# Causal attention: one visit for the values of a pair of heads, and the filling projections at other places

## The reference

```python
def mla_attention(c_q, c_kv, k_rope, q_norm, w_uq, kv_norm, w_ukv, cos, sin):
    q = (rmsnorm(c_q, q_norm) @ w_uq).reshape(b, s, MLA_HEADS, QK_NOPE + QK_ROPE)
    ...
    kv = (rmsnorm(c_kv, kv_norm) @ w_ukv).reshape(b, s, MLA_HEADS, QK_NOPE + V_DIM)
    k_nope, v = kv[..., :QK_NOPE], kv[..., QK_NOPE:]
    ...
    for i in range(s // Q_BLOCK):
        q0 = i * Q_BLOCK
        kend = q0 + Q_BLOCK
        sc = (jnp.einsum('bqhd,bkhd->bhqk', q_nope[:, q0:kend], k_nope[:, :kend])
              + jnp.einsum('bqhr,bkr->bhqk', q_pe[:, q0:kend], k_pe[:, :kend]))
        ...
        pr = jax.nn.softmax(jnp.where(mask, sc, -jnp.inf), axis=-1).astype(v.dtype)
        outs.append(jnp.einsum('bhqk,bkhd->bqhd', pr, v[:, :kend]))
```

## Time and profile before

| | us |
|---|---|
| median of 3 runs | 3806.12 (3800.87 to 3807.11) |
| profiled execution, its own time | 3797.35 |
| its span, first to last instruction | 3795.5 |
| TensorE busy in the span | 3663.5 |
| causal attention, layer 0, about | 201 to 341 |

### The profile page before, as it was taken

One profiled execution on the slowest core, in us unless ns is written; L12 is line 12 of the kernel. 1 busy time (PEld: TensorE's weight loads), 2 busy tenths in 40 slices (PEclk: granted clock), 3 DMA queues, 4 the chain that ended last, 5 costly groups with the idle time before them and its releaser, 6 DMA issues.

```text
span 3795.5 us, 58344 instructions
## 1 busy us (share of the span) xinstructions
PE 3663.5 (97%) x19742; PEld 2985.5 (79%) x19742; DVE 2165.3 (57%) x3292; ACT 1860.3 (49%) x3571; POOL 1772.5 (47%) x1395
## 2 busy tenths in 40 slices
PE   8999899999999988999999999999999999999999
PEld 7866688788888666887888887778888987678887
DVE  4567642788535676427885764742235957743234
ACT  4555544444445555444344545744444653754443
POOL 4423573556544235735565453065563235025564
PEclk9999999999999999999999999999999999999999
DMA  4210241455222102414553322132223542012222
GB/s 143 89 62 29 73 139 62 155 190 187 94 89 89 62 29 73 145 62 153 195 183 106 128 95 95 46 106 96 97 95 104 174 161 78 2 43 91 94 95 88
DMA packets 106907, 388.48 MB, mean 102 GB/s; under 512 B 11856, under 2 KB 11984, under 8 KB 106320
## 3 DMA queue, kind: packets, MB, share of 16 engines
q1 hardware_dynamic: 87840, 318.81, 24.5%
q10 hardware_dynamic: 16416, 57.62, 4.4%
q0 software_dynamic: 2448, 9.36, 0.7%
HBM read 383.64 MB, written 2.10 MB: 102 GB/s over the span
## 4 chain that ended last, share of the span: by engine, by line
PE 69%; issue 15%; DVE 7%; POOL 6%; ACT 2%; DMA 0%; POOLq 0%; ACTq 0%; DVEq 0%; SPq 0%
PE ps L676 18%; PE ps L678 18%; PE ps L677 18%; POOL arena_parts L640 3%; PE ps L1163 2%; POOL arena_parts L644 1%; PE ps L1182 1%; PE ps L1171 1%; DVE rstd L2135 1%; PE ps L2200 1%; POOL lines L431 1%; PE ps L1141 1%; PE ps L2210 1%; PE ps L907 1%; PE ps L848 1%
## 5 line engine op out<-in xcount | busy, mean ns | idle before, releaser
L677 PE MATMUL ps<-arena_parts 128*128 128x512 f32 (+1 forms) x3156 | 1174.3, 372 | 0.0
L640 POOL TENSOR_TENSOR arena_parts<-ring,arena_parts 128x512 fp32r<-128x512 f32 x492 | 655.5, 1332 | 1021.4 <-ACT arena_parts L617 817.8
L676 PE MATMUL ps<-h_parts,arena_parts 128*128 128x512 f32 x2096 | 822.8, 393 | 10.1 <-POOL arena_parts L640 7.2
L678 PE MATMUL ps<-h_parts,arena_parts 128*128 128x512 f32 x2096 | 816.6, 390 | 0.0
L644 POOL TENSOR_TENSOR arena_parts<-ring,arena_parts 128x512 fp32r<-128x512 f32 x492 | 664.7, 1351 | 282.2 <-ACT arena_parts L626 281.6
L677 PEld LDWEIGHTS ps<-arena_parts 128*128 128x128 f32 x3156 | 596.1, 189 | 104.3 <-issue 2.4
L1663 DVE SCALAR_TENSOR_TENSOR conv<-ps,cols,conv 128x511 f32<-128x511 f32 (+3 forms) x536 | 377.6, 705 | 525.0 <-ACT conv L1678 371.3
L617 ACT ACTIVATE arena_parts<-ring 128x512 fp32r<-128x512 f32 x574 | 361.2, 630 | 640.5 <-PE ps L678 595.0
L626 ACT ACTIVATE arena_parts<-ring 128x512 fp32r<-128x512 f32 x574 | 360.2, 628 | 589.4 <-PE ps L678 553.2
L676 PEld LDWEIGHTS ps<-h_parts,arena_parts 128*128 128x128 f32 x2096 | 394.3, 188 | 97.0 <-POOL arena_parts L640 8.1
L678 PEld LDWEIGHTS ps<-h_parts,arena_parts 128*128 128x128 f32 x2096 | 394.2, 188 | 82.4
(11 more groups left out here) (357 smaller groups left out, 6450.4 us busy)
## 6 DMA issues: line engine op xcount, KB each, us to landing
ring<-in_stream SPq DMA_DIRECT2D x606, 512.0 KB, 3.2
ctx<-in_mod ACTq DMA_DIRECT2D x48, 512.0 KB, 3.3
sq<-in_mod ACTq DMA_DIRECT2D x48, 512.0 KB, 3.3
sq<-in_bias POOLq DMA_DIRECT2D x8, 512.0 KB, 4.5
conv<-in_bias POOLq DMA_DIRECT2D x8, 512.0 KB, 4.5
arena<-in_mem ACTq DMA_DIRECT2D x2, 1024.0 KB, 4.7
out_y<-x ACTq DMA_DIRECT2D x8, 256.0 KB, 2.7
x<-in_x SPq DMA_DIRECT2D x4, 256.0 KB, 4.7
```

The costliest lines, as they stand in the source:

```text
L640: eng.tensor_tensor(side_of(lin, i, c, 0, to), side_of(lin, i, c, 0, raw), side_of(lin, i, c, 0, top), ALU.subtract)\
L676: pe.matmul(out, w_h, x_h, start=start, stop=False)
L677: pe.matmul(out, w_h, x_r, start=False, stop=False)
L678: return pe.matmul(out, w_r, x_h, start=False, stop=stop)
```

## The change

One visit now takes the values of all four blocks of a pair: at n = 1 of the next pair, behind the scores of its unit 4. Only the last pair still has visits of its own within it: blocks 0 and 1 at n = 5, block 2 at n = 7 and block 3 at the end. All visits come after the scores of unit u + 3, and no longer before them. Of the filling, q1 moves from n = 1 to n = 2 and v from n = 4 to n = 5; q0 and k stay. The turned probabilities of a pair now need a place of their own for each unit (`turned_probs`), two for units 0 and 1, and `copy` waits for the values of a whole pair before it writes a place again.

```diff
--- before.py
+++ after.py
@@ -1030,6 +1030,18 @@
         INV_NA = LAYERS * MEM_UNITS
         INV_SWA = INV_NA + PAIRS * NA_UNITS
 
+        def turned_probs(n, par):
+
+            flat = quarters[:, :, :].rearrange("p a b -> p (a b)")
+            if n == 0:
+                return cut(22752, P) if par else flat[:, 1920:2048]
+            if n == 1:
+                return cut(22880, P) if par else inv_row[:, :]
+            if n == 5:
+                return lead[:, 0:3 * P]
+            at = {2: 0, 3: 256, 6: 512, 7: 1024, 4: 1536}[n]
+            return flat[:, at:at + (n // 2 + 1) * P]
+
         class MlaUnit:
 
 
@@ -1044,7 +1056,7 @@
                 self.scores = ps[:, 3 + self.u % 3, 0:self.w]
                 self.turned = ps[:, 6 + self.u % 2, 0:self.w]
                 self.prob = conv[:, self.u % 4, 0:self.w]
-                self.probT = quarters[:, self.u % 4, 0:self.w]
+                self.probT = turned_probs(n, p % 2)
                 self.c = slice(self.u % 4, self.u % 4 + 1)
 
         FIRST_SPLIT = 2
@@ -1171,33 +1183,39 @@
                     mm = pe.transpose(un.turned[:, kk], un.prob[:, kk], ident)
                 mm.then_inc(S["pt_done"], 1)
 
-            def values(un, un2):
-
-                pe.wait_ge(S["pt_ready"], un2.at + 1)
-                if un.b == 0:
-                    pe.wait_ge(S["v_evac"], un.pair + 1)
-                    wait(pe, "o_evac", 2 * un.pair)
-                for kb in range(un.b + 1):
-                    for v in (un, un2):
-                        mm = pe.matmul(ps[heads_of(v.a), 2, un.b * P:un.w], vT[:, un.par * QB + kb, 2 * v.a * VD:2 * v.a * VD + VD],
-                                       v.probT[:, kb * P:(kb + 1) * P], start=kb == 0, stop=kb == un.b)
-                mm.then_inc(S["pv_done"], 2)
+            def values(p, blocks):
+
+                first, last = p * MLA_UNITS + 2 * blocks[0], p * MLA_UNITS + 2 * blocks[-1] + 1
+                pe.wait_ge(S["pt_ready"], units[last].at + 1)
+                if blocks[0] == 0:
+                    pe.wait_ge(S["v_evac"], units[first].pair + 1)
+                    wait(pe, "o_evac", 2 * units[first].pair)
+                for b in blocks:
+                    for kb in range(b + 1):
+                        for v in units[p * MLA_UNITS + 2 * b:p * MLA_UNITS + 2 * b + 2]:
+                            mm = pe.matmul(ps[heads_of(v.a), 2, b * P:v.w], vT[:, v.par * QB + kb, 2 * v.a * VD:2 * v.a * VD + VD],
+                                           v.probT[:, kb * P:(kb + 1) * P], start=kb == 0, stop=kb == b)
+                mm.then_inc(S["pv_done"], 2 * len(blocks))
 
             for un in units[:3]:
                 scores(un)
             for p in range(PAIRS):
                 q0, q1, k, v = mla_project(pe, l, p + 1, (p + 1) % 2)
-                fill = {0: q0, 1: q1, 3: k, 4: v} if p + 1 < PAIRS else {}
+                fill = {0: q0, 2: q1, 3: k, 5: v} if p + 1 < PAIRS else {}
                 for n in range(MLA_UNITS):
                     u = p * MLA_UNITS + n
-                    if n % 2 and u >= 3:
-                        values(units[u - 3], units[u - 2])
                     if u + 3 < len(units):
                         scores(units[u + 3])
+                    if n == 1 and p > 0:
+                        values(p - 1, range(QB))
+                    elif n == 5 and p == PAIRS - 1:
+                        values(p, range(QB - 2))
+                    elif n == 7 and p == PAIRS - 1:
+                        values(p, range(QB - 2, QB - 1))
                     turn(units[u])
                     if n in fill:
                         fill[n]()
-            values(units[-2], units[-1])
+            values(PAIRS - 1, range(QB - 1, QB))
 
         def mla_rope_dve(dve, l):
 
@@ -1291,8 +1309,10 @@
 
             def copy(un):
                 act.wait_ge(S["pt_done"], un.at + 1)
-                if un.u >= 4:
-                    act.wait_ge(S["pv_done"], U_MLA[l] + (un.u - 4) // 2 * 2 + 2)
+                p, n = divmod(un.u, MLA_UNITS)
+                back = 2 if n < 2 else 1
+                if p >= back:
+                    act.wait_ge(S["pv_done"], U_MLA[l] + (p - back + 1) * MLA_UNITS)
                 act.activation(un.probT, un.turned, ACT.Copy).then_inc(S["pt_ready"], 1)
 
             evac_k(0)
```

## The result

The changed kernel takes 3815.88 us (median of 7 runs, 3815.34 to 3822.22), the kernel before on the same chip 3802.47 us (7 runs). The ratio is 1.0038, with a 95% interval of 1.0028 to 1.0048: slower, by 13.4 us. Forecast were 3815 us, made as 8.7 us above a median of 3806.12. The range held, and the difference is half as large again as forecast. That the number itself is met within 1 us is luck: the median of before that it was added to lies 3.7 us above that of all seven executions, and the forecast difference 4.7 us under the measured one.

What follows compares the result with a forecast made beforehand. TensorE was taken to bound pairs with filling, the VectorE and ScalarE chain the last pair. Per layer +4.56 (middle pairs), -0.54 (first), +0.35 (last) gave +4.37; two layers +8.7, added to 3806.12: 3815 us, range 3800 to 3825.

Steps and rivals of the forecast that it cites:

- The wait for the keys: Before unit 8's scores, TensorE idles until ScalarE has copied the next pair's keys: 1.83 us in each pair with filling.
- The visit's price: Each visit to the values costs TensorE a fixed 0.35 us beyond its matmuls, taken for the change of array shape.
- The first part of the pair: Query projection to unit 4's turn: the remaining visit grows by 1.30 us, and another visit's 0.57 goes.
- It just fits ... For the sum: nothing: Late evacuation of v on ScalarE, then unit 8's softmax: 0.1 to 0.2 us of slack, so no cost added.
- second part of the pair: Unit 4's turn to the next query projection: 6.44 us before; two visits go, the 1.83 us wait comes.
- rival B: Late evacuation of v delays unit 8's softmax; next pair starts 0.5 us late, +16 us in all, 3822; chance 0.15.
- A: The forecast itself: the wait at unit 8's scores outweighs the visits saved, +5 to +13 us; chance 0.56.
- the visits' 1.07 us a pair: Middle pairs: three visits fewer, less the growth of the one left, save TensorE 1.07 us each.
- Pair 0: First pair of a layer: no visit left, so 2.37 us go and 1.83 of wait come, -0.54 us.
- The last pair: Pair without filling: the previous pair's values delay its chain, partly offset by an earlier idle time, +0.35 us.
- C: Wait and savings cancel, by earlier keys or a cheaper merged visit: -3 to +4 us, 3807; chance 0.14.
- D: Unit 8's scores don't wait, so only the visits' saving counts: -16.9 us, 3789; chance 0.15.

Runs made afterwards that it cites:

- e1: The changed kernel with the value projection back at n = 4, all else as changed: 3795.0 us, ratio 0.9983 to the kernel before.
- e3: The changed kernel with ScalarE's two copies of the keys placed ahead of its copy of unit 4: 3796.76 us, ratio 0.9982 to the kernel before.
- e2: The kernel before with only the new filling places (second query projection at n = 2, value projection at n = 5): 3813.46 us, ratio 1.0032.
- e4: The changed kernel with the visit of a whole pair cut in three, same matmuls: 3823.5 us, ratio 1.0055 to the kernel before.
- e8: The changed kernel with two of ScalarE's weight sections moved to n = 0 and 1 of the next pair: 3810.95 us, ratio 1.0020 to before.
- e9: The changed kernel with both moved projections at their old places (n = 1 and n = 4), so merged visits only: 3796.72 us, ratio 0.9987 to before.
- e6: The changed kernel with value projection back at n = 4 and two ScalarE weight sections moved into the next pair: 3788.72 us, ratio 0.9961 to before.

## Why the prediction was right, and where it was short

**The wait for the keys: right.** Forecast was that TensorE stands 1.83 us between the end of the turn of unit 4 and the scores of unit 8, 14 times. The trace has 2.24 us from turn to scores where I had 2.16, with 1.75 us of idle time where I had said about 1.6, 14 times. e1 takes the wait away and the kernel is faster than before, e3 cuts it to a third by moving nothing but ScalarE's two copies, e2 makes it in the kernel before.

**The visit's price: right in size.** 0.35 us read from start to start in one pair; 0.33 by e4. Its cause, the change of shape, stays argued. The first part of the pair, where TensorE is the bound, came out as summed: 10.99 + 1.30 - 0.57 = 11.72 us forecast, 11.67 measured.

**The step that failed: "It just fits ... For the sum: nothing".** For the second part of the pair I had 6.47 us (6.44 less 1.80 for the two visits in it, and 1.83 for the wait), it takes 6.85. I had counted the way of v's evacuation to the softmax of unit 8 and found 0.1 to 0.2 us of slack. The trace has four things that I hadn't. The scores of unit 8 come 0.08 us later than I had them and take 0.08 us longer to their successor, so that all behind them is 0.16 us late. ScalarE starts the evacuation of v 0.20 us behind the projection's successor (293.15 and 292.95), where I had let it start with it. The softmax's sum is thus read by +6.1 us from the turn of unit 4, and not by +5.8. And behind it stands VectorE's normalisation of unit 8, 0.55 us (294.40 to 294.95), which I had let end "as the turn is": the turn comes 0.13 us late by it, and the next query projection another 0.09 us.

The 0.16 us come in all 14 pairs with filling, the 0.22 us behind them only in the 12 of them in which ScalarE has sections to round: in pair 6, which has none, the turn of unit 8 is 0.43 us behind the scores. That is 2.24 + 2.64 = 4.9 us; the first part came out 0.05 us shorter in 12 middle pairs and each last pair 0.1 us shorter, which leaves 4.1 of the 4.4 us between the 8.7 forecast and the 13.1 of the attention. e8, which takes the sections out of that way, gives the 0.22 us back.

This is rival B's mechanism, and by my own sign for it (idle time before the turn of the next pair's unit 0, released by VectorE) it is there, at 0.22 us where B had 0.5. The chances took A and B for exclusive; the runs show A with a part of B, and the difference of 13.4 us lies at the top of A's +5 to +13.

**A saving that wasn't there to have.** The larger error is behind it, and the forecast hid it. I took the visits' 1.07 us a pair for saved wherever TensorE isn't made to wait for the keys. e1 has no such wait and yet a pair of 17.25 us and not 16.36. Before, TensorE needed 6.44 us from the turn of unit 4 on, and the two visits in it cost 1.8 of them. Without these it would need 4.64, but e1 shows that the way over ScalarE's queue takes 5.60 from the same point; so taking the visits out gave 0.84 us and not 1.8 before ScalarE was the bound. The 12.24 and 10.58 us of the whole pair say nothing of this; the bound changes within the pair. The forecast of the changed kernel was hurt by this only through the 0.38 us, since there TensorE waits in that half anyway; what I expected of e1 was off by 10 us. Merging alone (e9) gave 4.4 us of the 15 that 44 visits fewer at 0.35 us would make.

**Smaller terms.** Pair 0 was forecast at -0.54 us; from its first query projection to the next it takes 17.30 us against 17.44, -0.1, with the same 0.38 us in it. The last pair, forecast at +0.35, takes 13.80 us from the turn of unit 0 to the last copy against 13.55: +0.25. C (cancelling) and D (no wait) fall with the 14 waits.

**What stays open.** e2's time is some 7 us less than its profile says, e6's some 3 us less; in the other runs the attention's difference in the profile and that of the medians agree within 2.5 us. The granted clock is a lead: the mean of e2's six executions is 0.9857 and that of the 22 of before beside them 0.9846, and among these 22 an execution is some 1.9 us shorter for each 0.001 of clock. By this estimate some 2 of e2's 7 us are the clock; in e6 (0.9852 against 0.9844) it is some 1.7 of the 3. The rest was not settled.

## What to carry to other kernels

When work is moved on the engine that bounds a kernel, look for what it covered where it stood: here a projection of 1.88 us stood by its place between a turn and the scores that wait, over ScalarE, for that turn, and one step later it covered nothing. Read the other engines' slack for each half of a loop and not for the whole: ScalarE at 61% of the pair was the bound of 5.6 us of it as soon as TensorE needed less. And a saving on one engine may need the order of another mended before it shows: merging alone gave 0.13%, merging with two moves on ScalarE 0.38%, the two moves alone nothing.

## What the runs showed of the hardware

A visit on arrays of 128x64 between work on 128x128 costs 0.33 us beyond its matmuls, about 0.2 of them in the start-to-start times of its neighbours; it was measured by cutting one visit into three (e4). The change of the array's shape and back is the likely cause; no run shows it apart.

A wait costs TensorE a little more than itself: the scores of 128 columns take 0.30 us to their successor after 1.75 us of idle time (290.54 to 290.84) and 0.23 where nothing was waited for (292.95 to 293.18); in e3 they take 0.29 us after 0.57 us of idle time.

TensorE's granted clock stayed at 1.00 through the attention, although it now idles 1.75 us in each pair. Behind the attention it differs between the two profiles, in stretches that the change doesn't touch. The windows of the changed kernel, from 5.5 us after the last output's copy (granted clock third from the end):

```profile
351.30:356.30 5.00, 4.75 (x41) 4.36 (x40) 2.40 (x5) 3.04 (x5) 0.00 (x0) 1.00 0.02 5
356.30:361.30 5.00, 5.00 (x15) 2.09 (x14) 3.91 (x3) 3.54 (x6) 0.32 (x1) 0.90 0.00 0
361.30:366.30 5.00, 5.00 (x10) 2.66 (x9) 4.86 (x5) 5.00 (x19) 4.64 (x4) 0.50 0.00 0
366.30:371.30 5.00, 5.00 (x7) 1.69 (x6) 4.86 (x9) 2.28 (x5) 3.05 (x4) 0.50 0.00 0
```

From 361.30 on it is 0.50, which is the 1.2 GHz level against 2.4. The same instructions of the kernel before, 5.3 us earlier in its trace, had 0.66 and 0.68. In both, TensorE had been busy for 4.75 and then 5.00 of 5 us in the two windows before that.

It also differs between executions of one kernel. The 22 executions of the kernel before beside e1 to e4 go from 3796.78 us at a mean granted clock of 0.987 to 3806.66 us at 0.983, and the profiled execution of the changed kernel, the longest of its seven, has the lowest clock of them (0.982, the others 0.983 to 0.985). So the difference of two spans, here 24.9 us, is not the effect of an edit; that of the stage, 13.1 us, is.
